# The indexer's score products and top-value rounds, laid between the units of two gate blocks

## The reference, cut to what matters

```python
proj = x @ w_in
c_q, c_kv, k_idx, w_idx, gate = jnp.split(proj, [s1, s2, s3, s4], -1)
c_q = rms_norm(c_q, q_norm_g)
q_idx = (c_q @ w_idx_q).reshape(b, L, IDX_N_HEADS, IDX_HEAD_DIM)      # 16 heads of 64
...
s = jnp.einsum('bthd,bsd->bths', qi.astype(jnp.float32), k_idx_f)
score = jnp.einsum('bths,bth->bts', jax.nn.relu(s), wi) * idx_scale
score = jnp.where(causal[None], score, -jnp.inf)
_, sel = lax.top_k(score, k_top)                                       # k_top = 64
...
return (o * jax.nn.silu(gate)) @ w_out
```

## Time and profile before

| | us |
|---|---|
| median of 3 runs | 2195.86 (2195.33 to 2195.95) |
| the profiled execution | 2192.14 |
| its span, first to last instruction | 2190.5 |
| around the span | 1.64 |
| TensorE busy | 2081.5 (95%) |
| VectorE busy | 1388.9 (63%) |
| ScalarE busy | 1103.3 (50%) |
| mean granted clock of TensorE | 0.977 of full speed |

### The profile page before, as it was taken

The page is one execution under the profiler, slowest core; times in us unless marked ns, Lnnn a source line. Parts: engine busy times, 40 slices in busy tenths (PEclk is TensorE's granted clock), DMA queues, the critical chain, the costliest instruction groups (busy, mean ns, idle before and its releaser), DMA issues.

```text
span 2190.5 us, 30992 instructions
## 1 busy us (share of the span) xinstructions
PE 2081.5 (95%) x12246; PEld 1826.0 (83%) x12246; DVE 1388.9 (63%) x1775; ACT 1103.3 (50%) x1468; POOL 52.5 (2%) x60
## 2 busy tenths in 40 slices
PE   4889999999999998999999999999899999999996
PEld 3668888878889987899998788888789888998785
DVE  4774575557775656466676566667764755776555
ACT  5852455544443444344456667666444444775432
POOL 0000000000000000000000000001000000000001
PEclk8889999999999999999999899999999999999998
DMA  9942553338785565355555455555544455335552
GB/s 347 332 178 97 174 172 116 109 114 274 271 283 198 187 217 163 116 175 187 171 179 181 146 192 185 179 191 173 204 156 152 153 188 177 116 115 173 192 192 77
DMA packets 204807, 394.56 MB, mean 180 GB/s; under 512 B 6791, under 2 KB 25981, under 8 KB 202269
## 3 DMA queue, kind: packets, MB, share of 16 engines
q1 hardware_dynamic: 200736, 371.88, 50.8%
q0 software_dynamic: 2304, 15.30, 1.8%
q10 hardware_dynamic: 1660, 5.90, 0.7%
HBM read 390.89 MB, written 2.16 MB: 179 GB/s over the span
## 4 chain that ended last, share of the span: by engine, by line
PE 87%; DVE 6%; ACT 3%; DMA 2%; issue 2%; ACTq 0%; DVEq 0%; SPq 0%
PE ps L1919 13%; PE ps L1921 13%; PE ps L1920 12%; PE ps L1939 9%; PE ps L1931 8%; PE ps L1933 8%; PE ps L1932 8%; PE ps L1940 5%; DVE w_lo L1073 2%; ACT w_hi L467 2%; DMA tables<-in_tables 1%; PE ps L2124 1%; PE ps L2102 1%; DVE tables L1426 1%; PE ps L2310 1%
## 5 line engine op out<-in xcount | busy, mean ns | idle before, releaser
L1073 DVE TENSOR_TENSOR w_lo<-raw,w_hi 128x1024 fp32r<-128x1024 f32 (+1 forms) x676 | 813.1, 1221 | 622.1 <-ACT w_hi L467 620.7
L467 ACT ACTIVATE w_hi<-raw 128x1024 fp32r<-128x1024 f32 (+1 forms) x676 | 699.6, 1051 | 681.3 <-PE ps L1921 346.0
L1931 PE MATMUL ps<-act,w_hi 128*128 128x256 f32 x1152 | 332.6, 289 | 4.1 <-DVE w_lo L1073 3.2
L1933 PE MATMUL ps<-act,w_lo 128*128 128x256 f32 x1152 | 325.9, 283 | 0.0
L1932 PE MATMUL ps<-act,w_hi 128*128 128x256 f32 x1152 | 325.8, 283 | 0.0
L1939 PE MATMUL ps<-act,w_hi 128*128 128x512 f32 x896 | 316.1, 398 | 4.5 <-DVE w_lo L1073 3.2
L1919 PE MATMUL ps<-w_hi,act 128*128 128x512 f32 (+1 forms) x640 | 252.6, 395 | 8.3 <-issue 7.4
L1940 PE MATMUL ps<-act,w_lo 128*128 128x256 f32 x896 | 250.9, 280 | 0.0
L1921 PE MATMUL ps<-w_hi,act 128*128 128x512 f32 (+1 forms) x640 | 248.2, 388 | 0.0
L1920 PE MATMUL ps<-w_lo,act 128*128 128x512 f32 (+1 forms) x640 | 248.1, 388 | 0.0
L1919 PE MATMUL ps<-w_hi,gated 128*128 128x512 f32 x576 | 226.6, 393 | 2.3 <-DVE gated L1766 1.4
(11 more groups left out here) (289 smaller groups left out, 2809.2 us busy)
## 6 DMA issues: line engine op xcount, KB each, us to landing
raw<-in_ssd_w_in SPq DMA_DIRECT2D x80, 1024.0 KB, 5.2
raw<-in_w_in SPq DMA_DIRECT2D x72, 1024.0 KB, 5.3
raw<-in_w_ada SPq DMA_DIRECT2D x48, 1024.0 KB, 5.9
raw<-in_dsa_w_in SPq DMA_DIRECT2D x36, 1024.0 KB, 5.0
raw<-in_ssd_w_out SPq DMA_DIRECT2D x32, 1024.0 KB, 5.0
raw<-in_dsa_w_out SPq DMA_DIRECT2D x32, 1024.0 KB, 5.1
raw<-in_w_out SPq DMA_DIRECT2D x16, 1024.0 KB, 5.1
raw<-in_w_proj_a SPq DMA_DIRECT2D x12, 1024.0 KB, 5.1
```

The costliest lines, as they stand in the source:

```text
L467: e.activation(w_hi[:, nth(u) % SPLIT, :, :w], raw[:, t % RAW, 2 * h:2 * h + 2, :w], ACT.Copy).then_inc(hi_done, 1)
L1073: e.tensor_tensor(w_lo[:, slot, :, :w], raw[:, t % RAW, 2 * h:2 * h + 2, :w], w_hi[:, slot, :, :w].bitcast(F32), ALU.subtract).then_inc(lo ...
L1931: e.matmul(o, wh, hi, start=first and f % 2 == 0, stop=False, skip_group_check=True)
L1933: ins = e.matmul(o, wl, hi, start=False, stop=last and f % 2 == 1, skip_group_check=True)
```

## The change

Nothing is computed otherwise and no instruction is added to the arithmetic. The order on three queues changes:

- **TensorE.** After q3 comes g0; three heads' products follow each of g0 to g4 and the sixteenth head follows g5. Then g6, g7 and the second block come. The index queries now go to banks 4 to 7 and not 0 to 3, since block one takes 0 to 3. The wait for the first copy of the index queries stands at head 0, for the second at head 2.
- **ScalarE.** g0 is split ahead of the first copy, g1 and g2 ahead of the second, g3 behind it. In each of six turns a split (g4 to g9) is followed by up to three relus.
- **VectorE.** In each of six turns a split is followed by the adds of up to three heads. The mask, the splits of g10 and g11 and the halves of the first block follow; then each of the eight rounds stands behind one split (g12 to g19), and the halves of the second block and the bias stand behind the last round.
- Blocks three to six are written out on ScalarE and VectorE, in the same order as the loop had them.

```diff
@@ scalar @@
-            for n in range(2):
+            u0 = 2 * FIRST["lat_gate"]
+            def idx_read(n):
                 e.wait_ge(units_used, ready("idx_q", n))
                 e.activation(gatedf[:, n * 1024:(n + 1) * 1024].rearrange("p (b c) -> p b c", b=2),
-                             ps[:, 2 * n:2 * n + 2, :], ACT.Copy).then_inc(act_freed, 1)
-            splits(2 * FIRST["lat_gate"], 4)
-            for h in range(16):
+                             ps[:, 4 + 2 * n:6 + 2 * n, :], ACT.Copy).then_inc(act_freed, 1)
+            def idx_relu(h):
                 e.wait_ge(S["idx_scores"], h + 1)
...
-            segment("lat_gate", 4, 6, added_silu)
+            splits(u0, 1)
+            idx_read(0)
+            splits(u0 + 1, 2)
+            idx_read(1)
+            splits(u0 + 3, 1)
+            for m in range(6):
+                splits(u0 + 4 + m, 1)
+                for h in range(3 * m, min(3 * m + 3, 16)):
+                    idx_relu(h)
+            splits(u0 + 10, 2)
+            added_silu(0, 0)
+            splits(u0 + 12, 8)
+            added_silu(1, 1)
+            for i in range(1, 3):
+                for k in range(2):
+                    splits(u0 + 16 * i + 8 * k + 4, 8)
+                    added_silu(2 * i + k, k)
@@ vector @@
+            for m in range(6):
+                splits(u0 + 4 + m, 1)
+                for h in range(3 * m, min(3 * m + 3, 16)):
+                    idx_add(h)
+            e.wait_ge(S["idx_step"], 32)
+            for lo in (0, 256):
+                v = score[:, lo:lo + 128]
+                e.tensor_tensor(v, v, tables[:, T_UNSEEN:T_UNSEEN + 128], ALU.add).then_inc(S["idx_step"], 1)
+            splits(u0 + 10, 2)
+            late_added(0, 0)
+            for r in range(TOPK // 8):
+                splits(u0 + 12 + r, 1)
+                idx_round(r)
+            late_added(1, 1)
...
-            segment("lat_gate", 4, 6, add_halves("lat_gate", LO + 2048))
+            for i in range(1, 3):
+                for k in range(2):
+                    splits(u0 + 16 * i + 8 * k + 4, 8)
+                    late_added(2 * i + k, k)
@@ tensor @@
-                gemm(2 * FIRST["idx_q"] + 2 * b, 2, lat, 2 * b, False)
+                gemm(2 * FIRST["idx_q"] + 2 * b, 2, lat, 4 + 2 * b, False)
             e.wait_ge(S["idxk_ready"], 1)
-            e.wait_ge(act_freed, freed("idx_q", 1))
-            for h in range(16):
+
+            def idx_scores(h):
+                if h % 8 == 0:
+                    e.wait_ge(act_freed, freed("idx_q", h // 8))
+                if h == 2:
+                    e.wait_ge(act_freed, freed("idx_q", 1))
...
             def late_gate(b, k, i, u0, step):
+                if isinstance(b, int) and b == 0:
+                    for m in range(8):
+                        gemm(u0 + m, 1, act, 0, False, kc0=2 * m, starts=m == 0, ends=m == 7, wide=True)
+                        for h in range(3 * m, min(3 * m + 3, 16)):
+                            idx_scores(h)
+                    return
```

More of the change, by code:

```diff
@@ L1679, in _ @@
             splits(u0 + 10, 10)
-            splits(2 * FIRST["lat_gate"], 4)
+            u0 = 2 * FIRST["lat_gate"]
+            splits(u0, 4)
             score = side[:, 3072:3456]
@@ L1685, in _, with idx_add @@
             parts = ((0, 128), (128, 384))
-            for h in range(16):
+            late_added = add_halves("lat_gate", LO + 2048)
+            def idx_add(h):
                 e.wait_ge(S["idx_relu"], h + 1)
@@ L1697, in _, with idx_round @@
                     ins.then_inc(S["idx_step"], 1)
[L1698 to L1703, removed]
+            def idx_round(r):
                 for tt, (lo, hi) in enumerate(parts):
```

## The result

| | before | after |
|---|---|---|
| median | 2195.60 us (2195.16 to 2195.95, 4 runs) | 2182.95 us (2179.80 to 2185.47, 4 runs) |
| profiled execution | 2192.14 | 2184.95 |
| its span | 2190.5 | 2183.3 |

After over before is 0.9949, with a 95% interval of 0.9934 to 0.9965: 12.65 us less by the medians, faster, and inside the range. The forecast was 2183.6.

A forecast was written before the change was run, and what follows sets the result against it. TensorE, 87% of the chain, was taken as the bound. 22.19 (block) + 6.8 (products) + 1.2 (switches) = 30.2 us replaces 42.45, 12.3 less: 2195.86 - 12.3 = 2183.6 us median, range 2179.5 to 2188.5.

The forecast's parts named there:

- Waits taken away, no new ones: TensorE from q3 on: g0 starts with no gap, the 1.21 us wait goes, and helpers keep up without new waits.
- the stretch: From q3's end to g7's end, one gate block plus 16 heads' products: 42.45 us before, predicted 30.2.
- the products wait for relus: Rival in the first block: relus come late, five turns each give back some 2 us; near 2194 us, chance 0.04.
- The products, 16 heads in 6.8 us: TensorE, first block: fifteen heads at 0.41 us and a lone sixteenth at 0.66, together 6.8 us.
- Going in and out, 1.2 us: TensorE switching between gate matmuls and heads: six pairs at 0.2 us, 1.2 us in all, ends 0 and 2.4.
- the drained rival: First block: heads do not overlap and switches drain TensorE, 12.6 us; only 7.7 us less, 2188.2 us; chance 0.20.
- VectorE in the second block: Each split gets a round behind it, 21.5 of 22.19 us filled; rounds hidden, g20 ready 1.9 us ahead.
- The clock: With no wait left, TensorE's clock stays at 1.00 from q3 on; this gain is already within the 42.45 us.
- the slower rival: First block: interleaved 64-row products hold the clock at 0.50, costing 10 us more, 2206 us; chance 0.03.
- the forecast of 12.3: Whole kernel: first block with products takes 30.2 us in place of 42.45, so 12.3 us less.

The follow-up runs named there:

- e4: Changed kernel with all sixteen heads taking operands from rows 0 to 63, no alternating halves; q3's end to g7's end 35.27 us, one execution 2188.15 us.
- e2: Changed kernel with four heads behind each of g0 to g3 instead of three behind five units and one; median 2178.02 us, ratio to before 0.9928.
- e5: Changed kernel with all heads contracting over all 128 rows, so no switch of rows; q3's end to g7's end 32.74 us, one execution 2181.38 us.
- e8: Changed kernel with four extra VectorE instructions (4.9 us) ahead of the second block's halves; TensorE waited 2.90 us for g20; one execution 2186.70 us.
- e6: Changed kernel with products spread but the eight rounds and bias in one piece ahead of g10's split; median 2188.61 us, ratio to before 0.9975.
- e1: The changed kernel unaltered, timed once more; median 2179.86 us against 2194.70 before, ratio 0.9937; q3's end to g7's end 31.82 us.
- e3: Changed kernel with groups of 4, 2, 4, 2 and 4 heads behind g0 to g4; q3's end to g7's end 29.92 us, one execution 2180.52 us.
- e9: The kernel of e4 executed once more, unaltered; q3's end to g7's end 35.28 us, one execution 2186.70 us.

## Why the prediction was right, point by point

- **Waits taken away, no new ones:** right. None in the stretch after, and the first matmul of g0 follows q3 without a gap. Nor did the products wait for relus: that rival falls, even with groups of four.
- **The products, 16 heads in 6.8 us:** too little. They took 5 x 1.41 + 0.65 = 7.7. The step that failed is "in a run of three each head has a neighbour on the other half". Heads go in pairs: two in 0.76 us, the third alone in 0.65. The 0.41 a head was read from a run of four, which is two pairs; e4 shows the pairing go when the other half of the rows isn't used, and e2 shows what groups of an even number give back.
- **Going in and out, 1.2 us:** the mechanism right, the size too small: 0.32 a group, 1.9 in all, inside the ends I gave (0 and 2.4). e5 shows that it is the switch of rows. Both errors have one sign, and the stretch was 31.8 us where I had 30.2: 10.6 less and not 12.3, between the forecast and the drained rival. (That rival's sum counts 11 ways in and out where the plan has 12, 0.2 us that changes nothing here.)
- **VectorE in the second block:** right. The halves, which follow the last round, the splits of g20 to g22, and TensorE's first matmul of g20:

```profile
1752.86 2.28 DVE L1330 TENSOR_REDUCE gatedf<-ps 128x1024 f32<-128x2048 f32 x1
...
1757.22 3.50 DVE L1090 TENSOR_TENSOR w_lo<-raw,w_hi 128x1024 fp32r<-128x1024 f32 x3 [1.28 <-ACT w_hi L467]
```

```profile
1760.34 0.39 PE L1971 MATMUL ps<-act,w_hi 128*128 128x512 f32 x1
```

  g20's part was there about 1758.4 and TensorE took it at 1760.34: 1.9 us of slack, 1.9 predicted. e8 confirms it by using it up, e6 shows the price if the rounds are not spread.
- **The clock:** right in this stretch. It stayed at 1.00; the slower rival, that mixed products hold it down, falls.
- **The time:** the 12.65 us between the medians are nearer to the forecast of 12.3 than the mechanism is. The stretch gives 10.6. The interval of the ratio is 7.7 to 14.5 us less, so the other 2 us are within what executions scatter; e1 gave 14.8 with the same stretch. The forecast of the time was better than its reasons by that luck.

## What to carry to other kernels

A dependent side computation that stops the bounding engine is best cut into pieces that fit between the units of independent work, with the helpers' work moved in step; work out the tightest hand-over (here g20, 2 us) by hand, since a fill of 97% leaves it narrow. In these runs small matmuls on half of the rows were best grouped in even numbers, and in as few groups as the waits allow: each group pays for two switches.

## What I had not expected of the hardware

- Two 64-row heads on opposite halves ran together in 0.76 us, not in the 0.65 of one; a third gained nothing. Why it does not overlap with the second was not found.
- At a granted clock of 1.00 a gate unit took one of two times, 2.77 or 2.83 us, and kept it until a group of heads or a wait came between: 22.19 us for the second block's eight units in the kernel before, after, e1, e2, e3 and e5, 22.62 in e4, e9 and behind the wait in e8. Inside the first block the pace could change at each group: in the changed kernel the gate pairs were 0.353 us apart in g0 and 0.347 from g1 on, in e4 the two took turns from g0 to g5. The splits of g11 and g19 in e4:

```profile
1726.70 1.06 ACT L467 ACTIVATE w_hi<-raw 128x1024 fp32r<-128x1024 f32 x1 [1.70 <-PE ps L1972]
...
1749.33 1.06 ACT L467 ACTIVATE w_hi<-raw 128x1024 fp32r<-128x1024 f32 x1 [1.71 <-PE ps L1972]
```

  What sets the pace was not found. Over five blocks it is 2 us, as much as the regrouping of e2.
